# A float32 two-block transformer stack on one Trainium2 core: modulation vectors as products and sums on VectorE instead of matmuls

## What is computed

```python
def adaln_modulation(cond, w_ada, b_ada):
    return jnp.split(jax.nn.silu(cond) @ w_ada + b_ada, N_MOD, axis=-1)      # N_MOD = 9

def ffn_sublayer(x, shift, scale, gate, w_gu, w_down, g, b):
    y = swiglu(modulate(x, shift, scale), w_gu, w_down)
    return deepnorm_residual(x, MACARON_WEIGHT * gate * y, g, b)

for layer in range(DEPTH):                                                   # 2
    mods_lat = adaln_modulation(c, ada_w[layer], ada_b[layer])               # latent tokens
    mods_ctx = adaln_modulation(c_ctx, ada_w[layer], ada_b[layer])           # context tokens
    x   = ffn_sublayer(x,   *mods_lat[0:3], ...)
    ctx = ffn_sublayer(ctx, *mods_ctx[0:3], ...)
    o_lat, o_ctx = mixer(modulate(x, *mods_lat[3:5]), modulate(ctx, *mods_ctx[3:5]), ...)
    x = deepnorm_residual(x, mods_lat[5] * o_lat, ...)
    x = ffn_sublayer(x, *mods_lat[6:9], ...)
    if not last:
        ctx = deepnorm_residual(ctx, mods_ctx[5] * o_ctx, ...)
        ctx = ffn_sublayer(ctx, *mods_ctx[6:9], ...)
```

## Time and profile before

| | |
|---|---|
| median of 3 runs | 2997.11 us (2996.68 to 2999.16) |
| the profiled execution, its own time | 2999.68 us |
| its span in the trace | 2997.9 us, mean granted PE clock 0.955 |
| PE busy | 2799.8 us (93%), 17152 matmuls |
| DVE busy | 1595.1 us (53%), 2729 instructions |
| ACT busy | 1387.2 us (46%) |
| POOL busy | 687.5 us (23%) |
| DMA | 354.4 MB, mean 118 GB/s, `ring<-w_stream` 643 x 512 KB |
| low parts of the split on DVE, L2008 | x1068, 832.1 us |
| `ada` on PE, L1515 and L1516 | x240 each, 102.5 and 94.9 us |
| `ada_raw` on PE, L1524 | x64 and x32 records, two to a tile |

### The profile page before, as it was taken

The page is one execution under the profiler, slowest core; times in us unless marked ns, Lnnn a source line. Parts: engine busy times, 40 slices in busy tenths (PEclk is TensorE's granted clock), DMA queues, the critical chain, the costliest instruction groups (busy, mean ns, idle before and its releaser), DMA issues.

```text
span 2997.9 us, 43781 instructions
## 1 busy us (share of the span) xinstructions
PE 2799.8 (93%) x17152; PEld 2385.3 (80%) x17152; DVE 1595.1 (53%) x2729; ACT 1387.2 (46%) x2567; POOL 687.5 (23%) x624
## 2 busy tenths in 40 slices
PE   8999998987898899999999997889979999899998
PEld 5888886866676688887788886779979888898778
DVE  5554446778634554554533334565543556535666
ACT  4444445631114544444433334665545576445673
POOL 1110011012223211011211112121124433545324
PEclk9999998999889999999999997899979999999999
DMA  6444431210022244443222221225533433433324
GB/s 256 162 157 167 169 137 61 78 43 2 23 78 76 92 162 163 162 168 127 71 98 99 99 85 64 85 92 178 183 104 134 148 120 120 139 136 134 120 104 136
DMA packets 97869, 354.44 MB, mean 118 GB/s; under 512 B 10752, under 2 KB 12928, under 8 KB 97280
## 3 DMA queue, kind: packets, MB, share of 16 engines
q1 hardware_dynamic: 97664, 351.64, 33.6%
HBM read 350.55 MB, written 1.05 MB: 117 GB/s over the span
## 4 chain that ended last, share of the span: by engine, by line
PE 73%; DVE 11%; ACT 7%; issue 5%; POOL 3%; DMA 1%; SPq 0%; DVEq 0%; ACTq 0%; POOLq 0%
PE ps L1491 19%; PE ps L1493 18%; PE ps L1492 18%; ACT spl L1792 2%; PE ps L1515 2%; PE ps L1516 2%; DVE spl L2008 1%; PE ps L1524 1%; PE ps L1548 1%; DVE big L2198 1%; PE ps L1746 1%; DVE work L2093 1%; ACT X L1849 1%; PE ps L1542 1%; POOL bigr L2439 1%
## 5 line engine op out<-in xcount | busy, mean ns | idle before, releaser
L1491 PE MATMUL ps<-bigr,spl 128*128 128x256 f32 (+1 forms) x3880 | 1341.6, 346 | 68.4 <-POOL bigr L2439 33.2
L1492 PE MATMUL ps<-bigr,spl 128*128 128x256 f32 (+1 forms) x3880 | 1312.5, 338 | 0.0
L1493 PE MATMUL ps<-bigr,spl 128*128 128x256 f32 (+1 forms) x3880 | 1311.7, 338 | 0.0
L2008 DVE TENSOR_TENSOR spl<-ring,spl 128x512 fp32r<-128x512 f32 x1068 | 832.1, 802 | 892.2 <-ACT spl L1792 891.4
L1792 ACT ACTIVATE spl<-ring 128x512 fp32r<-128x512 f32 x1254 | 750.8, 625 | 805.8 <-PE ps L1493 736.4
L1491 PEld LDWEIGHTS ps<-bigr,spl 128*128 128x128 f32 x3880 | 748.6, 193 | 185.8 <-POOL bigr L2439 50.9
L1492 PEld LDWEIGHTS ps<-bigr,spl 128*128 128x128 f32 x3880 | 750.3, 193 | 76.5 <-issue 2.2
L1493 PEld LDWEIGHTS ps<-bigr,spl 128*128 128x128 f32 x3880 | 749.1, 193 | 77.0
L2439 POOL TENSOR_TENSOR bigr<-work,bigr 128x512 fp32r<-128x512 f32 (+1 forms) x200 | 210.3, 1057 | 1075.6 <-ACT bigr L1796 1075.3
L2434 POOL TENSOR_TENSOR spl<-ring,spl 128x512 fp32r<-128x512 f32 x186 | 253.9, 1367 | 361.8 <-ACT spl L1792 361.5
L1796 ACT ACTIVATE bigr<-work 128x512 fp32r<-128x512 f32 (+2 forms) x232 | 120.6, 522 | 230.9 <-DVE work L2070 79.3
(11 more groups left out here) (279 smaller groups left out, 2573.9 us busy)
## 6 DMA issues: line engine op xcount, KB each, us to landing
ring<-w_stream SPq DMA_DIRECT2D x643, 512.0 KB, 3.2
big<-w_stream SPq DMA_DIRECT2D x16, 512.0 KB, 11.2
X<-x_t SPq DMA_DIRECT2D x2, 1024.0 KB, 13.9
cst<-consts SPq DMA_DIRECT2D x1, 1601.5 KB, 9.6
X<-mem_t SPq DMA_DIRECT2D x1, 1024.0 KB, 5.8
out_t<-X SPq DMA_DIRECT2D x8, 128.0 KB, 2.1
prm<-params SPq DMA_DIRECT2D x1, 252.5 KB, 2.8
```

Source lines behind the costliest of these rows:

```text
L1491: pe.matmul(out, hi, x[0], start=k == 0, stop=False)
L1492: pe.matmul(out, hi, x[1], start=False, stop=False)
L1493: finish(pe.matmul(out, lo, x[0], start=False, stop=k == nk - 1), tile, key if k == nk - 1 else None)
L2008: dve.tensor_tensor(lo_half(h), raw_half(h), hi_half(h), SUB).then_inc(*sig("lo", h, by="lo_dve"))
```

## The change

Behind the first four groups, `ada_w` tiles are no longer split and no longer go through PE. Each is a raw half; DVE multiplies it by the condition's column (one scalar per partition) and adds it to an accumulator of 128 x 512, once for each of the two conditions (`ada_vec`). After eight tiles PE adds the accumulator up over partitions with eight matmuls of one column against ones (`ada_sum`), and DVE adds the bias (`ada_mod`). For vectors 5 to 8 of the last layer (groups 10 to 17) only the condition of the latents is computed. The scan pumps nothing any more. The work is dealt out anew: 12 groups (96 tiles) in ffn0, 10 groups (80 tiles) in ffn1, 10 groups (80) in ffn2, of which eight have one condition; the pumps are spread evenly over the 118 slots of a sublayer.

```diff
-NCH = 659
+NCH = 661
+SLOTS = 42 * 2 + 8 * 5 - 6
...
+            accs = Rot([(wk[7], wk[8]), (arow[:, 0:512], arow[:, 512:1024])])
...
                     if k % 4 == 3 and pos["auto"]:
-                        yield from pump()
+                        pos["slot"] += 1
+                        if pos["slot"] * pos["auto"] // SLOTS > (pos["slot"] - 1) * pos["auto"] // SLOTS:
+                            yield from pump()
...
+            def ada_vec(l, groups, conds=2):
+                prev = None
+                def total(g, acc, ai):
+                    bank, free, bi = banks.get()
+                    yield "ada_sum", l, g, acc, conds, bank, free
+                    accs.give(ai, ("ada_t", l, g))
+                    yield CUT
+                    yield "ada_mod", l, g, conds, bank
+                    banks.give(bi, ("mod", l, g))
+                for g in groups:
+                    acc, afree, ai = accs.get()
+                    for k in range(KD):
+                        tile = yield from take([("ada_w", (l,), 128 * k, 128, 512 * g, 512, 0)], 512, True)
+                        yield "ada_vec", l, g, k, acc, conds, tile, afree
+                        if k == 2 and prev:
+                            yield from total(*prev)
+                        yield CUT
+                    prev = g, acc, ai
+                yield CUT
+                yield from total(*prev)
...
                 keys = yield from decayed_keys(0)
-                pos["unsplit"] = True
...
-                    yield from pump()
...
-                    yield from pump()
...
-            gens.append(ada(0, range(4, 18)))
-            xs, ms = yield from ffn(0, T, xs, ms, ("ln_g00", "ln_b00"), ("ln_g00", "ln_b00", 0, 3, 4))
-            gens.append(ada(1, range(18)))
+            gens.append(ada_vec(0, range(4, 16)))
+            xs, ms = yield from ffn(0, T, xs, ms, ("ln_g00", "ln_b00"), ("ln_g00", "ln_b00", 0, 3, 4), 12 * 9)
             xs, ms = yield from even_mixer(xs, ms)
-            xs, ms = yield from ffn(1, T, xs, ms, ("ln_g02", "ln_b02"), ("ln_g02", "ln_b02", 1, 0, 1))
-            xs, ms = yield from ffn(2, T, xs, ms, ("ln_g10", "ln_b10"), ("ln_g10", "ln_b10", 1, 3, 4))
+            gens.append(ada_vec(0, range(16, 18)))
+            gens.append(ada_vec(1, range(8)))
+            xs, ms = yield from ffn(1, T, xs, ms, ("ln_g02", "ln_b02"), ("ln_g02", "ln_b02", 1, 0, 1), 10 * 9 + 2)
+            gens.append(ada_vec(1, range(8, 10)))
+            gens.append(ada_vec(1, range(10, 18), 1))
+            xs, ms = yield from ffn(2, T, xs, ms, ("ln_g10", "ln_b10"), ("ln_g10", "ln_b10", 1, 3, 4), 10 * 9 + 2)
...
+            def ada_sum(l, g, acc, conds, bank, free):
+                w.wait_ge(*done("ada_k", l, g, KD - 1))
+                for q in range(4):
+                    for s in range(conds):
+                        ins = pe.matmul(bank[:, 2 * q + s:2 * q + s + 1], acc[s][:, 128 * q:128 * q + 128], P("ones")[:, 0:1], start=True, stop=True)
...
+            def ada_vec(l, g, k, acc, conds, tile, free):
+                h = tile[0]
+                w.wait_ge(*done(*arrived(h)))
+                for s in range(conds):
+                    c = cs[:, 2 * k + s:2 * k + s + 1]
+                    if k == 0:
+                        ins = dve.tensor_scalar(acc[s], raw_half(h), c, None, MUL)
+                    else:
+                        if s == 0:
+                            w.wait_ge(*done("ada_k", l, g, k - 1))
+                        ins = dve.scalar_tensor_tensor(acc[s], raw_half(h), c, acc[s], MUL, ADD)
+                ins.then_inc(*sig("ada_k", l, g, k, by="used_dve", also=("used", h)))
```

More of the change, by code:

```diff
@@ L339, in order @@
             small_at[0] = small_top
-            pos = {"h": -1, "s": 0, "off": HC, "raw": False, "unsplit": False, "pool": False, "auto": False, "n": 0}
+            pos = {"h": -1, "s": 0, "off": HC, "raw": False, "unsplit": False, "pool": False, "auto": 0, "slot": 0, "n": 0}
             banks, tmps, sqs = Rot(PS), Rot(wk[0:3]), Rot(wk[3:5])
@@ L617, in ffn @@
                 hs = []
-                pos["auto"] = bool(gens)
+                pos["auto"], pos["slot"] = steps, 0
                 src = [(XM[k][0][:, 0:n], XM[k][1][:, 0:n], ms[k]) for k in range(KD)]
@@ L2048, in norm_cols @@
                     return
-                bb, gg = (P(x).unsqueeze(2).broadcast_to([128, 8, 2]) for x in (b, g))
+                bb, gg = (P(x).unsqueeze(2).broadcast_to(list(G.shape)) for x in (b, g))
                 linked()
@@ L2418, in vector_program @@
             run({f.__name__: f for f in (
-                tables, start, split, dual, ada_turn, acc_dve, moments, inverse, norm_cols, gate_cols, residual, glu, first_mod, ln_sub, ln_mul,
+                tables, start, split, dual, ada_turn, ada_vec, ada_mod, acc_dve, moments, inverse, norm_cols, gate_cols, residual, glu, first_mod, ln_sub, ln_mul,
                 ln_mod, ln_out, gates_in, gates_exp, gates_ratio, gates_series0, gates_series1, gates_series2, gates_scan, gates_back,
```

28 lines of the change are left out of this document (22 added, 6 removed).

## The result

The changed kernel takes **3563.73 us** (median of 4 runs, 3547.9 to 3568.11), against 2996.89 for the kernel before (4 runs): the ratio is 1.188, 95% interval 1.184 to 1.192. The forecast was 3432 with a range of 3300 to 3620, so direction and range hold; the loss is 567 us where 435 were expected.

A forecast was written before the change was run, and what follows sets the result against it. PE was taken to bound the sublayers before the change, a serial loop through DVE and the loads after it. 2997.9 us plus 470 for the sublayers minus 36 for the scan gave 3432 us, range 3300 to 3620.

The forecast's parts named there:

- What bounds the kernel, and the work removed and added: Sublayers: PE sets the time; PE loses 102 us, DVE gets 2.1 us per slot, under PE's 2.72.
- The turn: Sublayers: sums, load, ACT's copy and low part run serially per raw tile, 5.97 us each, 253 times.
- the prediction's three classes: Turns by what stands between raw tiles: 149 one split, 52 two halves of one chunk, 52 two chunks.
- The price of the second load: Sublayers: a second chunk's load within a turn adds 1.9 us, bounds 0.9 and 2.8, in 52 turns.
- The sum of the sublayers: ffn0, ffn1 and ffn2 together: 1677 us against 1207 before, +470 us.
- The scan: First mixer: without 16 pumps nothing later takes their place; 33 us saved there, 3 behind, 36 in all.
- The column sums: PE in the sublayers: 224 one-column matmuls, 27 us, hidden in PE's waits of some 3 us a turn.
- The ring hid no load (1): Rival for the sublayers: the three-slot ring hides loads, PE stays the bound, 2887 us; chance 3%.
- Rival 3: Sublayers: DVE runs ahead in half the turns, so the turn closes only in part, 3146 us; chance 7%.
- Rival 4: Sublayers: the turn happens to match PE's time now, 4.25 us, so no change; chance 1%.
- Rival 2: Sublayers: PE falls to the low clock and becomes the bound itself, 3878 us; chance 8%.
- The named checks: Changed profile: ffn0 pairs about 6.0 us apart, ACT load waits 830 us, PE under 70%, DMA about 100 GB/s.

The follow-up runs named there:

- experiment 1: Changed kernel with low parts made one chunk later (`NSLOT + 2` for `NSLOT + 1` in the limit on splitting ahead); 2976.35 us.
- experiment 2: Changed kernel with both conditions computed for the last eight groups too, 64 more products and sums on DVE; 3605.69 us.
- experiment 3: Changed kernel with one condition for all groups behind the first four, 192 fewer DVE operations, result not the reference's; 3433.6 us.
- experiment 5: Changed kernel with low parts one chunk later still than in experiment 1 (`NSLOT + 3`); 3096.15 us.
- experiment 11: Changed kernel with layer 1's first four groups through PE in the scan again (16 pumps), low parts as early as in the change; 3417.87 us.
- Experiment 4: Changed kernel with 16 fillers where the scan used to pump, each two float32 matmuls of 128 x 512 on constants; 3561.87 us.
- experiment 6: Changed kernel with low parts one chunk later and the scan's 16 pumps back for layer 1's first four groups; 2946.79 us.
- experiment 8: Kernel before the change without its 16 scan pumps, their 32 tiles going through PE in ffn1 instead; 3013.01 us.
- experiment 9: Changed kernel with low parts one chunk later and three buffers for low parts instead of four; 3013.49 us.
- experiment 7: Changed kernel with a ring of four chunks and three buffers for low parts instead of four, order rule unchanged; 3057.41 us.

## Why the prediction was right, and what it missed

**What bounds the kernel, and the work removed and added: right.** Moving 102 us from PE to DVE was no gain, because PE stopped being what the sublayers wait for. That the work itself would have been a gain is shown by experiment 1.

**The turn: right as a mechanism, and by experiments 1, 2, 3, 5 and 11 shown, not only argued.** Its price was 5.97 us; the median distance of the pairs in ffn0 is 6.1 (95 of them). Set beside the order of steps, the 253 distances fall into the prediction's three classes, with its counts of 149, 52 and 52. With one low part between and two conditions the median is 6.04 for 5.97, the load being a little longer (3.40 and 3.38 in the turns above, where 3.21 was taken); a second low part of the same chunk adds 0.57 for 0.60. A second chunk adds 2.4 us on the mean, for 1.9 within bounds of 0.9 and 2.8. The price of the second load was taken near the middle of two far bounds, and it turned out nearer to the upper one.

The Trainium skill ("DMA: Bandwidth & Descriptors", Latency and other measured facts) was drawn on for shorter loads at a lower rate. The prediction introduces it as speaking "for a longer load", which is a slip: its own next sentences say shorter. The traces bear out neither: the median load in ffn0 is 3.3 us at 96 GB/s, and it was 3.3 at 159.

**The sum of the sublayers was too low by 89 us**, 559 instead of 470. The turns measured from DVE's timeline are 615 + 530 + 500 = 1645 us against 1597: 48 more, of which 24 are in the 52 turns with a second chunk, 15 in the 149 plain ones and 8 in the 52 with a second low part. What lies outside of the turns is 121 us instead of 80. The slots behind the last raw tile and the start of each sublayer were counted at PE's undisturbed pace; that they begin with no low part in stock would fit, but wasn't tried.

**The scan: the step that failed.** "Without them nothing later is in their place ... The scan gives 36 us." It gave nothing; the scan became 9 us longer (1031.93 to 1148.29 is 116.4 us, before 107.6). The mixer as a whole is at +5 instead of -36. The pumps were on the chain with 12.7%, and taking them off did take 33 us of work off; but without them PE had the low clock, 0.50 up to 1118 us, and paid the 33 us back, and 9 more. I had the number: "at half the clock all eight would be 8 x 7.4 = 59 us more". It stood only as a bound, because the scan of before has PE busy throughout and a clock of 0.87 over its length, and I took the busy share for the reason. Experiment 4 shows that wide matmuls bring the clock back within the scan, and experiments 6 and 11 that the pumps do. How much of the 36 us is lost without them is partly chance: this kernel's scan comes in at the low clock, and in experiments 8 and 9, which come in at the full one, it is 12 us shorter than before. On the profiled span, 3558.4 us against a forecast of 3432, 89 us are the sublayers, 41 the mixer, 2 what follows ffn2, and -6 the layer norm between ffn1 and ffn2. The median lies another 5 us higher. That the total stayed within the range owes nothing to the middle figure: both errors point the same way, and the upper bound of 3599 had the low clock in the scan in it.

**The column sums** (L1578) are more than was counted: 28 groups of 16 records, not 14, since each float32 matmul is two records; at 1.68 us for 16 records, as they lie on the chain of experiment 1, that is 47 us, not 27. In the changed kernel they lie in PE's pauses, and L1578 isn't among the chain's lines of 1% and more, as forecast. In experiment 1, where PE is the bound, they hold 3.3% of ffn0's chain, 13 us; so they do cost something there, as the prediction's "without it they would cost" had it.

**The rivals.** The ring hid no load (1): the turn is 6.1 us, not 2. Rival 3, a turn that closes only in part, is what experiment 1 makes of it; in the changed kernel every one of the 253 places closed (the least distance is 5.1 us). Rival 4, no change, fell with the measured time. Rival 2, the low clock as the bound of the sublayers, came in part and without effect. PE's timeline between two turns of ffn0:

```profile
321.85 0.47 PE L1528 MATMUL ps<-bigr,spl 128*128 128x512 f32 x1 [3.20 <-DVE spl L2054]
322.15 0.40 PE L1529 MATMUL ps<-bigr,spl 128*128 128x512 f32 x1
...
323.39 0.63 PE L1528 MATMUL ps<-bigr,spl 128*128 128x512 f32 x1
...
325.53 0.63 PE L1530 MATMUL ps<-bigr,spl 128*128 128x512 f32 x1
...
327.86 0.50 PE L1528 MATMUL ps<-bigr,spl 128*128 128x512 f32 x1 [1.71 <-DVE spl L2054]
```

The clock goes down within a burst and is up again in the next, 0.87 on the mean; the slow burst ends 1.7 us before the next half is ready, so it fits in the turn, as the prediction argued. The Trainium skill's advice to keep the gaps between bursts short ("TensorE: Matmul & The Clock Gate", Why this matters for your kernels) holds as a direction: with a gap in each turn (3.20 and 1.71 us in these rows) the clock is 0.87 to 0.91 in the three sublayers, where it was 0.99 to 1.00. That every burst would run at half rate, as the prediction drew from it, the rows don't bear out: the burst behind the gap of 3.20 us begins at the full rate.

**The named checks.** Pairs in ffn0 6.1 us apart for 6.0: right. In ffn2's second part 5.3 was said; there the median is 5.8, as many turns hold a second low part or load, and 5.4 for the plain turns. ACT's waits for ring loads 1222 us in the whole run, 830 said for the turns alone. DMA in ffn0 96 GB/s for 100. PE's busy share in ffn0 is 73%, where "well under 70%" was said; a slow burst counts as busy for longer. A scan round of 7.4 us: wrong in the changed kernel (1031.93 to 1045.75 is 13.8), right in the first rounds of experiment 8.

## What to carry to other kernels

When an engine that runs in order both frees a place of a ring and later waits for what is loaded into that place, look for the work that stands behind the wait though its data has long arrived. A ring of three was worth a ring of one here, and one digit in the order was worth 587 us. Busy shares don't show this; listing one engine's order beside the loads' waits does. And before counting matmuls removed from a stretch as time, ask what the stretch's clock will be without them. When kernels are compared by their totals, look whether a stretch that should be equal is: the scan moved by up to 21 us here with the same work in it, and it made one forecast come true and hid half of another cost.

## What the hardware showed that was not expected

A busy PE doesn't keep its clock by being busy. In the scan PE runs back to back but for a pause of about 4 us ahead of the last round, where there are no wide matmuls. With float32 matmuls of 128 x 512 between the small ones the clock over the scan is 0.87 to 0.92; without them it is 0.57 to 0.72. In experiment 7 it fell among the scan's own small matmuls, 15 us into the scan, with no idle time of PE longer than 0.15 us before it:

```profile
858.10 1.00 PE L1757 MATMUL ps<-big,work 64*128 64x64 f32 x8
859.03 1.97 PE L1734 MATMUL ps<-big 128*64 128x128 f32 x8
```

At full clock the eight matmuls of L1734 take 1.09 us. So wide matmuls worth 30 us cost nothing against a scan that comes in at the low clock (102 to 108 us with them, 116 without), and 7 to 12 us against the shortest scan without them (95.4). What exactly the chip counts was not tried: fillers of another size, type or number weren't run.

The second of two loads in flight costs 2.4 us over one alone, as the mean of 52 turns. That is nearer to what three loads together had suggested (2.8) than to its time of issue (0.9). The turn at 414 us is one of the cheap ones: there the chain has `SPq L1467` for 0.33 us and then a load of 4.08, 1.3 more than a single load.
